# Four sums of weight blocks in the gate stage: made by GpSimd in the place of VectorE

## The reference

```python
u = rms_norm(h, g_mix[i])
z = u @ w_in[i]
q_a, k_a, v_a, q_b, k_b, v_b, f_b, gate_logits = jnp.split(z, SPLIT_POINTS, axis=-1)
y_a = sliding_window_attention(q_a, k_a, v_a, swa_sinks[i]) @ w_br_swa[i]
y_b = forgetting_attention(q_b, k_b, v_b, f_b + b_forget[i]) @ w_br_fox[i]
gates = jax.nn.sigmoid(gate_logits).reshape(B, S, N_BRANCH, D_MODEL)
mixed = gates[:, :, 0] * y_a + gates[:, :, 1] * y_b
```

## Time and profile before

| what | value |
|---|---|
| median of three runs | 1750.27 us (1748.89 to 1750.78) |
| the profiled execution | 1748.98 us, its span 1747.2 us |
| PE busy | 1719.8 us (98%) |
| DVE busy | 1164.4 us (67%) |
| ACT busy | 710.3 us (41%) |
| POOL busy | 258.7 us (15%) |

### The profile page before, as it was taken

How to read it: one execution, slowest core, us unless ns; L and a number is a source line. 1 busy time by engine, 2 the same in 40 slices (tenths; PEclk the granted TensorE clock), 3 DMA queues, 4 the chain that set the end, 5 groups by cost and what they waited for, 6 DMA issues and landing times.

```text
span 1747.2 us, 21038 instructions
## 1 busy us (share of the span) xinstructions
PE 1719.8 (98%) x8377; PEld 1448.7 (83%) x8377; DVE 1164.4 (67%) x1481; ACT 710.3 (41%) x1082; POOL 258.7 (15%) x318
## 2 busy tenths in 40 slices
PE   7999999999999999999999999999999999999997
PEld 7888887888998888888888888888888888888886
DVE  5653565544997866589848866984887356445497
ACT  4332466653996331543232323323344234222133
POOL 2000011102884215100000000000002132000101
PEclk9999999999999999999999999999999999999999
DMA  5678977797653781383182256227211113221032
GB/s 183 242 267 320 334 259 253 238 334 191 139 131 128 234 295 55 107 301 129 64 295 95 82 212 222 94 78 285 98 49 36 49 61 115 67 90 55 19 127 97
DMA packets 137746, 280.67 MB, mean 161 GB/s; under 512 B 9456, under 2 KB 29488, under 8 KB 134192
## 3 DMA queue, kind: packets, MB, share of 16 engines
q1 hardware_dynamic: 137648, 279.33, 47.0%
HBM read 212.16 MB, written 67.14 MB: 160 GB/s over the span
## 4 chain that ended last, share of the span: by engine, by line
PE 85%; DVE 7%; ACT 2%; issue 2%; DMA 1%; POOL 1%; SPq 0%; POOLq 0%; ACTq 0%; DVEq 0%
PE PS L748 13%; PE PS L750 13%; PE PS L749 13%; PE PS L995 11%; PE PS L997 11%; PE PS L996 11%; PE PS L724 3%; PE PS L887 2%; PE PS L888 2%; PE PS L889 2%; PE PS L1097 1%; PE PS L1098 1%; PE PS L1099 1%; PE PS L909 1%; POOL TF L2344 1%
## 5 line engine op out<-in xcount | busy, mean ns | idle before, releaser
L1107 ACT ACTIVATE WH<-WB 128x2048 fp32r<-128x2048 f32 x56 | 107.3, 1917 | 286.2 <-PE PS L997 239.2
L748 PE MATMUL PS<-UH,RHL 128*128 128x512 f32 (+1 forms) x512 | 191.1, 373 | 2.5 <-DVE UL L1552 2.2
L1552 DVE TENSOR_TENSOR WB<-WB,WH 128x2048 fp32r<-128x2048 f32 x56 | 128.2, 2290 | 97.3 <-ACT WH L1107 97.3
L750 PE MATMUL PS<-UH,RHL 128*128 128x512 f32 (+1 forms) x512 | 189.8, 371 | 0.0
L749 PE MATMUL PS<-UL,RHL 128*128 128x512 f32 (+1 forms) x512 | 189.8, 371 | 0.0
L995 PE MATMUL PS<-WH,AH 128*128 128x512 f32 x448 | 174.8, 390 | 1.0 <-DVE H L1915 0.5
L995 PE MATMUL PS<-AH,WH 128*128 128x512 f32 x448 | 174.6, 390 | 0.0
L997 PE MATMUL PS<-WH,AL 128*128 128x512 f32 x448 | 174.3, 389 | 0.0
L997 PE MATMUL PS<-AH,WB 128*128 128x512 f32 x448 | 174.3, 389 | 0.0
L996 PE MATMUL PS<-WB,AH 128*128 128x512 f32 x448 | 174.3, 389 | 0.0
L996 PE MATMUL PS<-AL,WH 128*128 128x512 f32 x448 | 174.3, 389 | 0.0
(11 more groups left out here) (270 smaller groups left out, 3835.0 us busy)
## 6 DMA issues: line engine op xcount, KB each, us to landing
WB<-in_w_ff SPq DMA_DIRECT2D x32, 1024.0 KB, 9.2
AH<-uf_scratch SPq DMA_DIRECT2D x21, 1024.0 KB, 5.3
AL<-uf_scratch SPq DMA_DIRECT2D x21, 1024.0 KB, 7.4
GX<-gates_scratch SPq DMA_DIRECT2D x64, 256.0 KB, 3.5
gates_scratch<-GST SPq DMA_DIRECT2D x56, 256.0 KB, 4.0
H<-in_x SPq DMA_DIRECT2D x16, 512.0 KB, 8.8
RAW<-in_w_in SPq DMA_DIRECT2D x16, 512.0 KB, 7.3
UH<-ugT_scratch SPq DMA_DIRECT2D x8, 1024.0 KB, 7.4
```

Of the source, the lines that this page charges most:

```text
L748: pe.matmul(o_ap, sh, mh, start=first, stop=False)
L750: ins = pe.matmul(o_ap, sl, mh, start=False, stop=last)
L1107: return act.activation(dst, src, ACT.Copy, **more)
L1552: return dve.tensor_tensor(dst, src, high.bitcast(F32), ALU.subtract)
```

## The change

The four sums of unit 1 move from VectorE to GpSimd. There each stands directly behind a scaling: S1 behind that of window 3, S3 behind window 4's, S2 behind window 5's, S4 behind window 6's. Their operands and places are the same. Since another engine now writes the places, each sum has a further wait, for the low parts (`gw_low`) that were the last to be made from what it overwrites. The semaphore of the sums is split in one for each unit. The sums of unit 0 stay on VectorE, and so do all low parts.

```diff
-        gw_sum = signal("gw_sum", [(u, n) for u in range(2) for n in ("S1", "S3", "S2", "S4")])
+        gw_sums = [signal(f"gw_sum{u}", [(n,) for n in ("S1", "S3", "S2", "S4")]) for u in range(2)]
...
             def gate_low(n, m):
                 if n:
-                    on.wait_ge(*gw_sum.of(g_order[n][0], "S4"))
+                    on.wait_ge(*gw_sums[g_order[n][0]].of("S4"))
...
             for n in g_steps:
                 for k in range(8):
                     if k in (1, 3) and n < 13:
-                        if n == 6 and k == 1:
-                            gate_wide_sum(1, "S4")
                         gate_low(n + 1, k // 2)
-                    if n == 4 and k in (5, 7):
-                        gate_wide_sum(1, "S1" if k == 5 else "S3")
-                    if n == 5 and k == 5:
-                        gate_wide_sum(1, "S2")
...
-            for step in swa_steps:
+            def gate_wide_sum(name):
+
+                at_, (dst, a, b, op) = g_place[1], g_wide_sums[name]
+                for v in {"S1": ("A21", "A22"), "S3": ("A11",), "S2": (), "S4": ("A12",)}[name]:
+                    on.wait_ge(*gw_in[v].of(1))
+                if name != "S1":
+                    on.wait_ge(*gw_sums[1].of({"S3": "S1", "S2": "S3", "S4": "S2"}[name]))
+                on.wait_ge(*gate_sum.of({"S1": 3, "S3": 3, "S2": 4, "S4": 5}[name], 3))
+                on.wait_ge(*gw_low.of(*{"S1": (4, 1), "S3": (4, 1), "S2": (5, 1), "S4": (6, 1)}[name]))
+                pool.tensor_tensor(g_spot[0][at_[dst]], g_spot[0][at_[a]], g_spot[0][at_[b]], op).then_inc(*gw_sums[1].up(name))
+
+            for n, step in enumerate(swa_steps):
                 for v in step:
                     window(*v)
+                    if v[0] == "norm" and 3 <= v[1] < 7:
+                        gate_wide_sum(("S1", "S3", "S2", "S4")[v[1] - 3])
```

More of the change, by code:

```diff
@@ L350, in build @@
                    {"A11": "R5", "A12": "d", "A21": "R0", "A22": "R3", "S1": "a", "S3": "R0", "S2": "c", "S4": "R2"}]
+        g_wide_sums = {"S1": ("S1", "A21", "A22", ALU.add), "S3": ("S3", "A11", "A21", ALU.subtract),
+                       "S2": ("S2", "S1", "A11", ALU.subtract), "S4": ("S4", "A12", "S2", ALU.subtract)}
         g_spot = []
@@ L1195, in gate_high @@
                 name = g_wide[p]
-                on.wait_ge(*(gw_in[name].of(u) if name[0] == "A" else gw_sum.of(u, name)))
+                on.wait_ge(*(gw_in[name].of(u) if name[0] == "A" else gw_sums[u].of(name)))
                 on.wait_ge(*(used[S_kb.idx[1 if n == 0 else 3]] if n < 3 else gate_sum.of(n - 2, 3)))
@@ L1681, in turned_low @@
                 less(TUL[:, t_place[name], :, :], TU[:, t_place[name], :, :], TH).then_inc(*t_low.up(name))
[L1683 to L1687, removed]
+            def gate_wide_sum(name):
+                at_, (dst, a, b, op) = g_place[0], g_wide_sums[name]
                 for v in {"S1": ("A21", "A22"), "S3": ("A11",), "S2": (), "S4": ("A12",)}[name]:
-                    on.wait_ge(*gw_in[v].of(u))
+                    on.wait_ge(*gw_in[v].of(0))
                 if name != "S1":
[L1691 to L1694, removed]
+                    on.wait_ge(*gw_sums[0].of({"S3": "S1", "S2": "S3", "S4": "S2"}[name]))
+                dve.tensor_tensor(g_spot[0][at_[dst]], g_spot[0][at_[a]], g_spot[0][at_[b]], op).then_inc(*gw_sums[0].up(name))
             def gate_low(n, m):
                 if n:
-                    on.wait_ge(*gw_sum.of(g_order[n][0], "S4"))
+                    on.wait_ge(*gw_sums[g_order[n][0]].of("S4"))
                 else:
@@ L1718, in vector @@
             for name in ("S1", "S3", "S2"):
-                gate_wide_sum(0, name)
+                gate_wide_sum(name)
             projected("kb", 1)
-            gate_wide_sum(0, "S4")
+            gate_wide_sum("S4")
             def window(kind, i, r):
```

## The result

| | median | range | runs |
|---|---|---|---|
| before | 1749.97 us | 1748.19 to 1750.90 | 22 |
| after | 1752.51 us | 1751.32 to 1754.26 | 22 |

The ratio, which is estimated from all executions and so isn't exactly the quotient of the medians, is 1.0015, with a 95% interval of 1.0009 to 1.0021: some 2.6 us slower. That is surely more than nothing.

What follows compares the result with a forecast made beforehand. TensorE, busy 98% of the span, was taken as the bound, so only its few gate-stage waits mattered. The four steps summed to +3.6 us on a three-run median of 1750.27, forecasting 1753.9 us, range 1750.8 to 1756.0.

Steps and rivals of the forecast that it cites:

- the chain's own range: Main case, VectorE held through all four sums: +3.6 us, own range 1753.1 to 1755.2 us, chance 0.76.
- Price of a sum: Each moved sum on GpSimd takes 4.61 us, with bounds of 3.8 and 5.41 us.
- Step 1, S1: Behind window 3's scaling: S1 holds gate_low(5, 0) 3.21 us late; TensorE newly waits 1.6 us for PRL.
- Step 2, S3: Behind window 4's scaling: window 5's maximum comes 2.54 us late; TensorE waits 0.6 us more, 2.2 in all.
- Step 3, S2: Behind window 5's scaling: gate_low(6, 1) goes first, then S2; window 6's maximum 2.07 us late, TensorE hardly waits.
- S2 takes the port first: Rival: S2 goes before gate_low(6, 1), making the addition behind it 7.3 us late: 1757.6 us; chance 0.05.
- nothing is held: Rival: two-operand VectorE instructions pass beside GpSimd and VectorE gains: about -0.6 us, 1749.7 us; chance 0.05.
- Step 4, S4: Behind window 6's scaling: gate_low(7, 0) waits for S4; TensorE gets PRL at 277.7 instead of 274.06, +3.6 us.
- From here both orders are the same: After S4: window 7's biases and queries' DMA 3.6 us late, TensorE's 0.76 us wait recurs, lateness carried to the end.
- not held: Rival: VectorE's tiny 128x4 instructions in each window are not delayed by GpSimd's sums: +1.1 us, 1751.4 us; chance 0.12.

Runs made afterwards that it cites:

- e2: Only S1 on GpSimd, the other three sums on VectorE as before, against the kernel before: 1752.28 us, ratio 1.0011.
- e1: Changed kernel with each moved sum replaced by three GpSimd fills that read nothing from SBUF, against the kernel before: 1750.26 us, ratio 1.0000.
- e7: Only S2 on GpSimd, the other three sums on VectorE as before, against the kernel before: 1749.43 us, ratio 0.9998.
- e3: Only S4 on GpSimd, the other three sums on VectorE as before, against the kernel before: 1752.12 us, ratio 1.0009.
- e4: Changed kernel with step 7's low halves made two eighths later on VectorE, against the kernel before: 1752.26 us, ratio 1.0015.
- e11: Changed kernel with three quarters of step 7's two token loads left out, against the kernel before: 1752.93 us, ratio 1.0018.
- e10: Kernel before with three quarters of step 7's two token loads left out, against the kernel before: 1749.36 us, ratio 0.9998.
- e6: Kernel before, all sums on VectorE, with only step 7's low halves two eighths later, against the kernel before: 1749.88 us, ratio 1.0002.
- e12: Changed kernel with each GpSimd sum half its size and the other half a fill, against the kernel before: 1748.48 us, ratio 0.9994.
- e8: Changed kernel with each GpSimd sum split into two instructions of half the size, against the kernel before: 1752.11 us, ratio 1.0012.

## Why the prediction came out as it did

The forecast was 1753.9, the median 1752.51 us: inside the range of 1750.8 to 1756.0, a difference under 0.2%, where the text had put nearly as much chance as above it, and below the chain's own range of 1753.1 to 1755.2. The mechanism stood; its size was too large.

- **Price of a sum.** 4.61 us, as worked out from the earlier trace rows, three times; S2's 5.59 is its wait for gate_low(6, 1) and 4.48 us of work (260.23 to 264.71). The lower end, 3.8, and the upper, 5.41, are out. The 5.41 was never a price: in the earlier trace rows VectorE's difference ends at 655.37 + 4.66 = 660.03 and GpSimd's second sum at 659.10 + 5.41 = 664.51, again 4.48 us of work behind a wait.
- **Step 1, S1.** Right: gate_low(5, 0) held to 241.81 (forecast: 3.21 us late; 241.81 - 238.92 + 0.13 for the earlier trace = 3.02), a new wait for PRL near 246 us of 1.22 us (forecast 1.6; by the starts 1.43 us late, 246.63 - 245.33 + 0.13, because a wait shows only from the recorded end of the matmul before). e2 shows this sum alone doing it, e1 that it is the reading.
- **Step 2, S3.** The maximum is held, 2.92 us (forecast "3"). The further wait of 0.6 us did not show as a wait, as TensorE's transposes of window 5 came at 256.57 without one over 0.2; a further lateness of 0.33 us is there (256.57 - 254.94 + 0.13 = 1.76 us, where the forecast had 2.2).
- **Step 3, S2.** The order was right: gate_low(6, 1) first, then S2, and the maximum of window 6 held, 1.58 us. The rival *S2 takes the port first* is refuted by 258.23 + 2.00: the difference ended 1.07 us after the scaling. That S2 by itself gains, which the rival *nothing is held* named, was true in e7 (-0.79 us), through the biases that no longer stand behind it; that nothing is held was not (1.59 us).
- **Step 4, S4.** The wait at window 6's transposes is the one forecast; e3 has it from S4 alone, e4 without S4 in front of PRL has not.
- **The term that was mis-sized** is the sum over these links, +3.6 us, measured +2.76. Lateness of the links, forecast and measured (with the 0.13 us by which the later trace is earlier): scaling of window 4 1.39 and 1.20, of window 5 2.54 and 2.06, of window 6 2.07 and 1.27, the low half of step 7 3.69 and 2.75. Each link came out 0.14 to 0.32 us shorter than I made it. I laid the recorded durations end to end, with 0.07 us between. The rows show them overlap: S1 starts at 236.12, before the scaling's recorded end at 236.17, and a held instruction ends 1.08 (a 1.22 us one) or 0.01 us (a 0.17 us one) behind its releaser, not its full length behind. The earlier trace rows had that 1.08 in them, and the prediction quoted it and then added 1.22. Over four links that is 0.94 us. The chain's own range is loose as well: +3.2 to +4.8 on 1750.27 are 1753.5 to 1755.1, not 1753.1 to 1755.2.
- **"From here both orders are the same".** Nearly: the queries' wait took 0.25 us back (0.51 in place of 0.76 us; in e11 and e10, with less ahead of the queries, 0.75 and 0.73), and the rest stood at +2.4 to the end of the last stage but one. The remainder of the 1.4 us between forecast and median is the base, 1750.27 from three runs against 1749.97 from 22.
- **The tiny instructions.** The rival *not held* (1751.4) is refuted by 2.92 and 1.58 us; size doesn't exempt an instruction of 128x4.
- **What the prediction didn't see.** It called VectorE's waits the ones to be gained or lost and the queries' DMA a thing that follows. e4 to e6 show that the DMAs are a second limit 12 us on: where the queries come to be asked for closer behind the token load, what is gained at window 6 is mostly not kept. Where they do not, it is kept (e7 -0.79 and -0.66 us, e12 -1.67 and -1.72). Nor did it see that TensorE's new wait of 2.3 us can be followed by a lower granted clock (e1, e3, e8); that the profile after doesn't have it is luck.

## What to carry to other kernels

Before moving an instruction from VectorE to GpSimd, list which of VectorE's instructions beside its new place have two operands in SBUF, or are a TENSOR_SCALAR of the kind held here; each waits for its end, however small, and whatever stands behind them in order waits too. Ask also what waits by semaphore for the moved instruction itself: half of the loss here was that S4 came later. Where several such moves hang on one another (each ends on the chain of the next), their length is paid several times (4.43 us for 1.29 in e12), and a move in pieces lets the held ones in. When a wait is removed, look at once for the next transfer whose issue hangs on it, at what was issued right ahead of it, and at how full the DMA engines are where it would now run.

## What the runs showed of the hardware beyond that

- A fill on GpSimd (128x2048, 1.81 us) holds VectorE's TENSOR_SCALAR of 128x4 to its end (0.17 to 1.31, 1.79, 1.32 us) but not a TENSOR_TENSOR of two SBUF operands (1.22 us kept, e1). A half sum on GpSimd holds such a TENSOR_SCALAR too (2.32 us in e8).
- GpSimd's instruction that is next in order lets VectorE's waiting one go first: S2 took 5.59 us in the record for 4.48 of work, and in e8 the pair of halves 5.75 us where VectorE's difference came in between, 4.76 where none did.
- Full DMA engines carry different rates: 397 GB/s at a share of 1.05 while token loads run (270 to 274 us), 236 and 256 at 1.01 while the queries' later pieces run with stores and other loads (278 to 286 us).
- After the same wait of 2.0 us near 1705 us, TensorE's granted clock fell, to 0.83 to 0.87 in one of the two stretches of 10 us from 1700 on, in 7 of 14 profiles (after's among them), and stayed at 1.00 in the others (before's among them). It makes 1.6 us, two thirds of what was to be measured here. After a wait of 2.31 to 2.42 us near 275 us it fell in 3 of 5 profiles (e1, e3, e8; not in after and e11).
